# Moving the first expert tile's gate-up product ahead of the shared expert's turns and down products

## What is computed

```python
def moe(h, lp):                      # h: 384 x 1024
    ...                              # sigmoid router, 2 of 4 groups, the best 4 of 32 experts, weights w
    gu = jnp.einsum('nd,edf->nef', t, lp['w_exp_gu'])          # 32 experts, 1024 -> 2 x 256
    a = jax.nn.silu(gu[..., :EXPERT_FF]) * gu[..., EXPERT_FF:]
    a = (a * combine[..., None].astype(a.dtype)).reshape(-1, N_EXPERTS * EXPERT_FF)
    routed = a @ lp['w_exp_down'].reshape(N_EXPERTS * EXPERT_FF, D_MODEL)
    sgu = t @ lp['w_sh_gu']                                    # the shared expert, all tokens
    shared = (jax.nn.silu(sgu[:, :SHARED_FF]) * sgu[:, SHARED_FF:]) @ lp['w_sh_down']
    return (routed + shared).reshape(B, T, D)
```

## Time and profile before

| | us |
|---|---|
| median of 3 runs | 2106.28 |
| lowest and highest | 2102.24, 2112.89 |
| the profiled execution | 2108.57 |
| its span, first to last instruction | 2106.4 |
| busy in it: PE, DVE, ACT, POOL | 1884.7, 1283.1, 1040.4, 451.5 |
| mean granted clock of TensorE, as a share of full speed | 0.948 |

### The profile page before, as it was taken

How to read it: one execution, slowest core, us unless ns; L and a number is a source line. 1 busy time by engine, 2 the same in 40 slices (tenths; PEclk the granted TensorE clock), 3 DMA queues, 4 the chain that set the end, 5 groups by cost and what they waited for, 6 DMA issues and landing times. The chain is left out here.

```text
span 2106.4 us, 27239 instructions
## 1 busy us (share of the span) xinstructions
PE 1884.7 (89%) x9282; PEld 1393.5 (66%) x9282; DVE 1283.1 (61%) x1827; ACT 1040.4 (49%) x1713; POOL 451.5 (21%) x422
## 2 busy tenths in 40 slices
PE   4999899899998999999649999979999799999991
PEld 2987566788877566666438865668888666666661
DVE  2244567644436688888753455675444467888885
ACT  2333235633335478777533412464333437787782
POOL 0001511310000434444200043114000042343430
PEclk8999999999998999999869999999999989999996
DMA  7534464133334599999834434503333248999984
GB/s 259 175 120 123 154 226 156 47 120 120 121 109 181 178 359 354 345 348 347 295 99 143 136 118 143 200 6 98 123 120 120 106 174 309 355 351 339 350 313 177
DMA packets 145349, 416.91 MB, mean 198 GB/s; under 512 B 26704, under 2 KB 37232, under 8 KB 119152
## 3 DMA queue, kind: packets, MB, share of 16 engines
q1 hardware_dynamic: 125136, 379.76, 51.8%
q0 software_dynamic: 17952, 33.74, 4.8%
q10 hardware_dynamic: 2176, 2.27, 0.4%
HBM read 408.80 MB, written 32.15 MB: 209 GB/s over the span
## 5 line engine op out<-in xcount | busy, mean ns | idle before, releaser
L1648 DVE TENSOR_TENSOR W_split<-W,W_split 128x2048 fp32r<-128x2048 f32 (+2 forms) x92 | 216.2, 2352 | 423.8 <-ACT W_split L1253 423.8
L2190 PE MATMUL psum<-W_split,qT_split 128*128 128x512 f32 (+3 forms) x1536 | 411.4, 380 | 16.2 <-PEq L2519 8.0
L1253 ACT ACTIVATE W_split<-W 128x2048 fp32r<-128x2048 f32 (+2 forms) x92 | 170.0, 1854 | 385.2 <-PE psum L2190 385.2
L2190 PEld LDWEIGHTS psum<-W_split,qT_split 128*128 128x128 f32 x1536 | 284.7, 190 | 71.8 <-issue 16.5
L2190 PE MATMUL psum<-W_split,scratch_split 128*128 128x512 f32 x864 | 280.7, 396 | 0.0
L2190 PE MATMUL psum<-W_split,hT_split 128*128 128x512 f32 x576 | 214.6, 400 | 5.8 <-DVE scratch_split L1843 5.8
L2461 PE MATMUL psum<-W_split,zf_split 128*96 128x512 f32 x512 | 202.8, 396 | 0.0
L2190 PEld LDWEIGHTS psum<-W_split,scratch_split 128*128 128x128 f32 x864 | 162.4, 189 | 38.7
L2190 PE MATMUL psum<-W_split,kT_split 128*128 128x512 f32 (+3 forms) x480 | 177.7, 370 | 0.0
L1173 POOL DMA_INDIRECT zf<-token_rows,vm x56 | 123.6, 2206 | 48.4 <-POOL vm L1170 48.4
L2190 PEld LDWEIGHTS psum<-W_split,hT_split 128*128 128x128 f32 x576 | 109.7, 191 | 31.8 <-DVE scratch_split L1843 6.3
(11 more groups left out here) (353 smaller groups left out, 3872.0 us busy)
## 6 DMA issues: line engine op xcount, KB each, us to landing
W<-in_w_exp_gu SPq DMA_DIRECT2D x128, 1024.0 KB, 11.6
W<-in_w_exp_down SPq DMA_DIRECT2D x64, 1024.0 KB, 11.2
W<-in_w_in SPq DMA_DIRECT2D x60, 1024.0 KB, 5.1
W<-in_w_mod SPq DMA_DIRECT2D x40, 1024.0 KB, 5.3
W<-in_w_br SPq DMA_DIRECT2D x16, 1024.0 KB, 5.1
zf<-y_rows SPq DMA_DIRECT2D x12, 1024.0 KB, 7.1
W<-in_w_out SPq DMA_DIRECT2D x8, 1024.0 KB, 5.1
W<-in_w_mod SPq DMA_DIRECT2D x3, 2048.0 KB, 17.1
```

What stands on the lines that cost most here:

```text
L1253: nc.scalar.activation(high(j), piece(SPLITS[j]), ACT.Copy).then_inc(S["high_ready"], 1)
L1648: V.tensor_tensor(piece(SPLITS[j], Wr), piece(SPLITS[j]), high(j).bitcast(F32), ALU.subtract).then_inc(S["low_ready"], 1)
L2190: ins = nc.tensor.matmul(bank(job, piece_size(key)[1]), act_part[:, k0 + k, t * P:(t + 1) * P], w_part[:, k, :], start=first and (k, i) == ...
```

## The change

PE runs the transposes and the gate-up of expert tile 0 right behind the shared gate-up, and the shared turns and down products after it; the transposes of expert tile 1 come last. ACT and DVE follow: Silu and product of tile 0 come ahead of the shared copies. On DVE the low parts for tile 0, `product_shared(2)`, the product of tile 0 and the three shared copies now stand ahead of the table, and the low parts of expert 1 and tile 1 behind it. SP loads both gate-up halves of expert 2 ahead of expert 1's down matrix. Because the shared tiles now live on while tile 0's product is formed, they move to other memory, and the PSUM banks are dealt anew.

```diff
@@ plan_jobs: numbers, takers and banks of the planned PSUM jobs @@
+    for h in range(2):
+        jobs.add(("xt", 0, h), "dve", BANK_XT + h)
+    jobs.add(("gu", 0), "dve", BANK_GU)
+    jobs.add(("aT", "s", 0), "act", 4)
     for t in range(T):
-        if t == 0:
-            jobs.add(("aT", "s", 0), "act", 2)
         if t < T - 1:
-            jobs.add(("aT", "s", t + 1), "act", (5, 2)[t])
-        jobs.add(("y", "s", t, 0), "dve", (3, 6, 3)[t])
-        jobs.add(("y", "s", t, 1), "act", (4, 7, 4)[t])
-        if t != 1:
-            for h in range(2):
-                jobs.add(("xt", t // 2, h), "dve", BANK_XT + h)
-    jobs.add(("gu", 0), "dve", BANK_GU)
+            jobs.add(("aT", "s", t + 1), "act", (5, 4)[t])
+        jobs.add(("y", "s", t, 0), "dve", (3, 7, 6)[t])
+        jobs.add(("y", "s", t, 1), "act", (6, 3, 7)[t])
+    for h in range(2):
+        jobs.add(("xt", 1, h), "dve", BANK_XT + h)
@@ trunk: two tiles @@
-        shared = zf[:, 6144:6912].rearrange("p (t n) -> p t n", t=T)
-        shared_T = zf[:, 6912:7680].rearrange("p (t f n) -> p t f n", t=T, f=2)
+        shared = kT[:, 3 * D:3 * D + T * FF].rearrange("p (t n) -> p t n", t=T)
+        shared_T = PTb[:, :].rearrange("p (t f n) -> p t f n", t=T, f=2)
@@ SP @@
                     load_gate_up(1, expert("w_exp_gu", 1))
-                    sp.wait_ge(*filled(("y", "s", T - 1, 1)))
-                    load_down(1, expert("w_exp_down", 1))
                     sp.sem_inc(S["gu_half"], 2)
                     sp.wait_ge(S["gu_half"], 3)
                     load_half(0, 0, expert("w_exp_gu", 2))
                     sp.wait_ge(*filled(("gu", 0)))
                     load_half(0, 1, expert("w_exp_gu", 2))
+                    sp.wait_ge(*filled(("y", "s", T - 1, 1)))
+                    load_down(1, expert("w_exp_down", 1))
@@ ACT @@
                     silu_shared(2)
-                    turned_shared(0)
-                    empty_shared(0)
                     act.wait_ge(*filled(("xt", 0, 1)))
                     x_high(0)
-                    for t in (1, 2):
+                    act.wait_ge(*filled(("gu", 0)))
+                    nc.scalar.activation(silu[0:CAP, 0, :], psum[0:CAP, BANK_GU, 0:FF], ACT.Silu).then_inc(S["silu_ready"], 1)
+                    turned_shared(0)
+                    for t in range(T):
                         empty_shared(t)
...
                     x_high(1)
-                    act.wait_ge(*filled(("gu", 0)))
-                    nc.scalar.activation(silu[0:CAP, 0, :], psum[0:CAP, BANK_GU, 0:FF], ACT.Silu).then_inc(S["silu_ready"], 1)
@@ DVE (the definitions of gu_low, x_low, dn_low and empty_shared move up with their calls) @@
                     product_shared(1)
+                    gu_low(0, 0, 1)
+                    product_shared(2)
+                    gu_low(0, 1, 2)
+                    x_low(0, 1)
+                    dn_low(0, 3)
+                    product(BANK_GU, 0, T + 1)
+                    empty_shared(0)
+                    empty_shared(1)
+                    empty_shared(2)
                     within = zf[:, 12800:12800 + NE * (MORE + 1)].rearrange("p (j e) -> p j e", e=NE)
...
                     V.tensor_copy(turns_u, turns_f).then_inc(S["tables_ready"], 1)
                     dve.wait_ge(S["tables_ready"], 1)
-                    gu_low(0, 0, 1)
-                    product_shared(2)
-                    gu_low(0, 1, 2)
-                    empty_shared(0)
-                    x_low(0, 1)
-                    dn_low(0, 3)
-                    empty_shared(1)
-                    empty_shared(2)
                     gu_low(1, 0, 3)
                     gu_low(1, 1, 4)
                     x_low(1, 3)
-                    product(BANK_GU, 0, T + 1)
@@ PE @@
+                    def turn_first_rows(i):
+
+                        pe.wait_ge(S[f"x_landed{i}"], 16)
+                        for h in range(2):
+                            bank_free(("xt", i, h))
+                        turn_gathered(i)
+
+                    turn_first_rows(0)
+                    pe.wait_ge(*emptied(("xt", 0, 0)))
+                    pe.wait_ge(*emptied(("xt", 0, 1)))
+                    bank_free(("gu", 0))
+                    gate_up(0, 5)
                     turn_shared(0)
                     for t in range(T):
                         if t < T - 1:
                             turn_shared(t + 1)
                         down_shared(t)
-                        if t != 1:
-                            pe.wait_ge(S[f"x_landed{t // 2}"], 16)
-                            for h in range(2):
-                                bank_free(("xt", t // 2, h))
-                            turn_gathered(t // 2)
-                    pe.wait_ge(*emptied(("xt", 0, 0)))
-                    pe.wait_ge(*emptied(("xt", 0, 1)))
-                    bank_free(("gu", 0))
-                    gate_up(0, 5)
+                    turn_first_rows(1)
```

More of the change, by code:

```diff
@@ L2022, in _ @@
                     product_shared(1)
[L2024 to L2039, removed]
                     def gu_low(e, h, high_at):
@@ L2067, in _ @@
                     gu_low(0, 1, 2)
-                    empty_shared(0)
                     x_low(0, 1)
                     dn_low(0, 3)
+                    product(BANK_GU, 0, T + 1)
+                    empty_shared(0)
                     empty_shared(1)
                     empty_shared(2)
+                    within = zf[:, 12800:12800 + NE * (MORE + 1)].rearrange("p (j e) -> p j e", e=NE)
+                    below = zf[:, 13312:13312 + NE * (MORE + 1)].rearrange("p (j e) -> p j e", e=NE)
+                    shape = [P, MORE + 1, NE]
+                    j = iota[:, 0:MORE + 1, None].to_broadcast(shape)
+                    link(V.tensor_tensor(within, row_base[:, None, :].to_broadcast(shape), j, ALU.is_le))
+                    link(V.tensor_tensor(below, row_end[:, None, :].to_broadcast(shape), j, ALU.is_gt))
+                    link(V.tensor_tensor(within, within, below, ALU.mult))
+                    link(V.tensor_tensor(within, within, iota[:, None, :].to_broadcast(shape), ALU.mult))
+                    link(V.tensor_copy(expert_f[:, 0:NE], iota))
+                    link(V.tensor_reduce(expert_f[:, NE:NT], within, AX, ALU.add))
+                    link(V.tensor_scalar(tmp[:, 0, 0:NT // 2 - NE // 2], iota[:, 0:MORE + 1:2], row_end[:, NE - 1:NE], None, ALU.is_lt))
+                    link(V.tensor_reduce(turns_f, tmp[:, 0, 0:NT // 2 - NE // 2], AX, ALU.add))
+                    link(V.tensor_scalar(turns_f, turns_f, float(NE // 2), None, ALU.add))
+                    V.tensor_copy(expert_u, expert_f)
+                    V.tensor_copy(turns_u, turns_f).then_inc(S["tables_ready"], 1)
+                    dve.wait_ge(S["tables_ready"], 1)
                     gu_low(1, 0, 3)
```

## The result

The changed kernel takes 2128.61 us at the median (2127.62 to 2129.72) beside 2106.34 us for the kernel before: ratio 1.0102, 95% interval 1.0077 to 1.0126. The change made the kernel slower by 22 us. The profiled execution took 2127.62 us with a span of 2125.8 us.

The account below looks back on a forecast made before the run. A DMA-full loop whose loads start when PE starts it was taken as the bound. Start shift 10.3 plus clock 2.2 gave 12.5 us per layer, +25.0 over two: 2106.3 to 2131.3 us, range 2120 to 2138, wider 2115 to 2140.

Parts of the forecast that it names:

- Steps 1 to 3: Ahead of the loop: PE gaps of 0.8 and 2.4 us, tile 0's gate-up ending at 707.2, down_shared(0) starting at 708.0 us.
- Step 4: Shared down products: DVE starts emptying the last one's first half 9.1 us after they begin, at 717.1 us; copy ends 717.8.
- Steps 5 and 6: DVE behind the last shared copy: table 4.97 us, to 722.8 us, then expert 1's splits and x_low(1) 5.43 us, to 728.2.
- Step 7: PE ahead of the loop: waits for all banks, reads number of turns, 1.25 us; starts at 729.45 for 719.12, shift 10.3 us.
- Step 8: TensorE's clock: 2.2 us more per layer for a first gate-up at half clock; the loop's own slow start unchanged, 0.
- The edits priced at nothing: Moved memory of two small tiles, SP's new load order, later reading of the turns by SP, POOL and ACT: 0 us.
- Rival (a): Ahead of the loop: expert 2's earlier loads fill idle DMA, gain 2 x 8.5 = 17 us, 2089 us; chance 0.06.
- Rival (b): In the loop: later, DMA-bound tiles make up half or more of the delay, +0 to +10 us, about 2112 us; chance 0.08.
- Rival (c): TensorE's clock stays up: +20.6 us, 2127 us; no chance of its own, counted within the forecast's 0.80.
- (d): Ahead of the loop: half clock into the down products and slower hand-offs, 16.3 us per layer, 2139 us; chance 0.06.
- One of the signs: Ahead of the loop: DMA share near 0 between 711 and 718 us, low again until the loop's first load at about 737.

Follow-up runs that it names:

- e1: Changed kernel with only the tile table moved on DVE from behind the last shared copy into the idle stretch behind dn_low(0); 2129.75 us.
- e7: e6 with PE reading the number of turns right behind tile 0's gate-up, ahead of the third shared turn and down product; 2097.22 us.
- e5: Changed kernel with SP's order of before: expert 1's down matrix loaded ahead of both gate-up halves of expert 2; 2128.94 us.
- e6: Kernel before with tile 1's transposes and tile 0's gate-up between second and third shared down product, table and expert 0 splits unmoved; 2100.15 us.
- e2: Changed kernel with expert 1's gate-up splits early, on ACT behind x_high(0) and on DVE behind dn_low(0); table unmoved; 2121.86 us.
- e3: Changed kernel with expert 1's splits early and the table on DVE between the first and second shared copy; 2114.09 us.
- e8: e3 with gu_low(0,1) on DVE ahead of product_shared(2); 2110.26 us.
- e4: Kernel before with only the table moved on DVE, behind its last shared copy; 2108.15 us.

## Why the prediction was right

The direction, the mechanism and the size were right: +25.0 us forecast, +22.3 us measured at the medians, inside the range of 2115 to 2140 us. The profiled execution alone came out 19.1 us longer, 6.0 us under its forecast of 2133.6 us; its second loop was 2.8 us shorter than that of the kernel before, and no run here shows why. By its steps, counted from the end of the shared gate-up, since the entry began 1.2 us earlier in this execution:

- Steps 1 to 3: gate-up forecast at 701.4 - 697.3 = 4.1 us, measured 4.1; gaps forecast 0.8 and 2.4 us, measured 1.02 and 2.23. The first shared down product forecast at 10.7 us with the clock up; measured 10.6 us in the second layer (1749.76 - 1739.17), where it stayed up (1.00 over the gate-up), and 12.2 in the first, where it fell (0.76).
- Step 4: 9.1 us to DVE's last copy, measured 717.41 - 708.30 = 9.1.
- Steps 5 and 6: the table 4.97 us, measured 722.78 - 718.02 = 4.8; splits and x_low(1) 5.4 us, measured 728.20 - 722.78 = 5.4. The prediction named DVE's chain as the bound with ACT done near 724 us; x_high ended at 724.1. What it did not say is how near ACT's chain lies behind DVE's: e1 shows that of the table's 5 us only 1.2 could be won back by moving the table alone.
- Step 7: 1.25 us, measured 1.26. That it contains the reading of the number of turns is shown by e7.
- Step 8 was the **mis-sized term**: 2.2 us in each layer for a first gate-up at half clock. No run shows 2.2 us for this gate-up. The figure is that of the loop's first gate-up in the kernel before, 7.8 us at a mean granted clock of 0.69, for the 5.6 us of one at 1.00, and the fall itself was expected from the 0.50 behind a gap of 2.36 us. In the changed kernel the gate-up of tile 0 took 7.2 us for 5.6 in the first layer, 1.6 us, and 5.6 us in the second, none. That is 1.6 us for the 4.4 forecast, about the whole miss of 2.7 us. With the clock's part left out, the forecast was 20.6 us. PE's start of the loop, counted from the end of the shared gate-up, moved by 11.5 - 1.6 = 9.9 us in the first layer and by 9.9 us in the second: 19.8 us.
- The edits priced at nothing cost nothing that shows: e5 says so for SP's order. e6 has the moved tiles too, and its time follows its path within 0.4 us. POOL's and ACT's later reading of the number of turns was not tried apart; the path explains the time without it.
- Rival (a), earlier loads: expert 2's halves did leave 8 us earlier and the DMA share did rise from 0.49 to 0.75, but the loop's first load was issued at 736.56 us, 9.8 us later than before (726.79 us), and e5 shows the early loads to be worth nothing: DMA's next load waited for PE, which began the loop's first gate-up only at 731.03 us. Rival (b), that the loop makes up part of the delay, is answered by the table: nothing is made up. Rival (c) came true in one layer of the two, (d) in neither. Its 1.8 us for the down products was an estimate, half of a product of about 3.6 us, and no run shows it: the first one behind the gate-up took 3.70 us in both layers, as in the kernel before.
- One of the signs failed: DMA was to be near idle from 711 to 718 us. Its share was 0.87 up to 714 us, since expert 2's second half was issued only at 707.59 us and a half took 6.5 us from issue to landing, and 0.01 from there to 718 us. The time does not hang on it.

## What to carry to other kernels

Where a full loop asks for its own loads, its start is the number to forecast: take every engine's list between the last shared work and the loop, add up each chain, and look for the second longest too, for it is what a repair of the longest uncovers. Work that has no user before the loop (here the table and the splits) belongs in an engine's idle stretch ahead of the last waited-for copy, not behind it. Moving a product ahead pays only if something else is left to cover the wait behind it: e6 and e7 move it ahead by one down product instead of three, and are faster than both kernels.

## What was not expected of the hardware

The granted clock did not follow the length of the gap just behind it. Behind 2.23 us of idle, with eight transposes and another 1.02 us of idle ahead of it, the granted clock fell to 0.50 of full speed in the first layer (700.40 to 703.80 us) and stayed at 1.00 in the second (1743.27 to 1748.85 us), in the same execution. Over the profiles of the changed kernel, e1, e2, e3 and e5, all with this pair of gaps, it fell in 6 of 10 entries: in all 5 first layers, but in the second layer only in e3. In e8, with 1.02 and 1.68 us, it fell in 2 of 2. Over the gate-up of tile 0 the mean was 0.67 to 0.76 where it fell and 1.00 where it did not. Ahead of the loop, behind 19.5 us of matmuls with one gap of 0.30 us among them, gaps of 2.66 to 2.88 us in e3 and e8 were followed by a fall in none of 4 cases; the gaps of 3.28 to 9.71 us there, in the kernel before, the changed one, e1, e2, e4 and e5, in all 12 (mean over the loop's first gate-up 0.69 to 0.86, and 1.00 in the 4). Why the layers differ stays open. A forecast does better to take a fall behind such a pair of gaps as likely and not as certain; one fall cost 1.6 us, and 2.4 us in the first layer of e1.
